# State-space heads of a two-block network: decay rows fetched from memory and differenced on GpSimd in place of a TensorE product and a ScalarE pass

## The reference

```python
a_cum = jnp.cumsum(a, axis=-1)                       # a = dt * A, per head, <= 0
seg = a_cum[..., :, None] - a_cum[..., None, :]
decay = jnp.exp(jnp.where(lower, seg, -jnp.inf))
y_diag = jnp.einsum('bcqgn,bcsgn,bgrcqs,bcsgrp->bcqgrp', cm, bm, decay, xs)
# + the part carried from the other chunk; then the same on the flipped sequence
y = y_fwd + y_bwd + d_skip[:, None] * xs
y = y * silu(z);  return rmsnorm(y, norm_w)
```

## Time and profile before

| what | value |
|---|---|
| median of 3 runs | 2441.19 us (2440.38 to 2445.71) |
| the profiled execution: its own time | 2443.01 us |
| its span | 2441.1 us |
| TensorE busy, mean granted clock | 2391.5 us (98%), 0.994 |
| VectorE, ScalarE, GpSimd busy | 1713.4, 1339.5, 90.2 us |

### The profile page before, as it was taken

One profiled execution on the slowest core, in us unless ns is written; L12 is line 12 of the kernel. 1 busy time (PEld: TensorE's weight loads), 2 busy tenths in 40 slices (PEclk: granted clock), 3 DMA queues, 4 the chain that ended last, 5 costly groups with the idle time before them and its releaser, 6 DMA issues.

```text
span 2441.1 us, 48177 instructions
## 1 busy us (share of the span) xinstructions
PE 2391.5 (98%) x18842; PEld 2289.4 (94%) x18842; DVE 1713.4 (70%) x2517; ACT 1339.5 (55%) x2355; POOL 90.2 (4%) x101
## 2 busy tenths in 40 slices
PE   9999999999999999999999999999999999999998
PEld 8898999999899999999999997899999999789998
DVE  7788777777888867786766575676566657667665
ACT  6788655644678855563444445554444444555443
POOL 0000000000100000000100010010001001001000
PEclk9999999999999999999999999999999999999999
DMA  7454555455354455545455553345545544434553
GB/s 216 131 159 126 165 164 161 154 170 189 108 153 139 137 156 160 169 155 181 145 181 174 169 160 106 121 144 178 170 147 179 178 163 152 123 124 142 189 181 113
DMA packets 401046, 380.19 MB, mean 156 GB/s; under 512 B 28223, under 2 KB 397037, under 8 KB 400765
## 3 DMA queue, kind: packets, MB, share of 16 engines
q1 hardware_dynamic: 397821, 373.87, 48.0%
q10 hardware_dynamic: 3072, 4.20, 0.7%
HBM read 372.77 MB, written 1.05 MB: 153 GB/s over the span
## 4 chain that ended last, share of the span: by engine, by line
PE 79%; DVE 12%; ACT 3%; DVEq 3%; issue 1%; SPq 1%; DMA 1%; ACTq 0%
PE ps L583 22%; PE ps L585 21%; PE ps L584 21%; DVE scratch L1806 3%; DVE w_lo L1583 3%; DVEq L1805 2%; PE ps L805 2%; PE ps L836 1%; PE ps L837 1%; PE ps L838 1%; ACT scratch L1082 1%; ACT w_hi L1082 1%; PE ps L854 1%; PE ps L612 1%; PE ps L614 1%
## 5 line engine op out<-in xcount | busy, mean ns | idle before, releaser
L1583 DVE TENSOR_TENSOR w_lo<-raw,w_hi 128x1024 fp32r<-128x1024 f32 x664 | 812.0, 1229 | 423.2 <-ACT w_hi L1082 421.8
L583 PE MATMUL ps<-x_hi,w_hi 128*128 128x256 f32 (+1 forms) x3664 | 1056.4, 288 | 4.3 <-DVE w_lo L1583 1.6
L584 PE MATMUL ps<-x_lo,w_hi 128*128 128x256 f32 (+1 forms) x3664 | 1042.6, 285 | 0.0
L585 PE MATMUL ps<-x_hi,w_lo 128*128 128x256 f32 (+1 forms) x3664 | 1039.8, 284 | 0.0
L1082 ACT ACTIVATE w_hi<-raw 128x1024 fp32r<-128x1024 f32 x664 | 697.7, 1056 | 447.5 <-PE ps L585 370.6
L583 PEld LDWEIGHTS ps<-x_hi,w_hi 128*128 128x128 f32 x3664 | 690.8, 189 | 30.8 <-issue 25.3
L584 PEld LDWEIGHTS ps<-x_lo,w_hi 128*128 128x128 f32 x3664 | 692.2, 189 | 2.0
L585 PEld LDWEIGHTS ps<-x_hi,w_lo 128*128 128x128 f32 x3664 | 693.6, 189 | 0.0
L583 PE MATMUL ps<-big_r,w_hi 128*128 128x272 f32 (+1 forms) x832 | 238.9, 287 | 0.0
L585 PE MATMUL ps<-big_r,w_lo 128*128 128x272 f32 (+1 forms) x832 | 238.2, 286 | 0.0
L1082 ACT ACTIVATE scratch<-ps 128x256 f32<-128x256 f32 (+9 forms) x328 | 122.3, 384 | 154.9 <-PE ps L838 63.8
(11 more groups left out here) (302 smaller groups left out, 3063.1 us busy)
## 6 DMA issues: line engine op xcount, KB each, us to landing
raw<-in_w_in SPq DMA_DIRECT2D x184, 512.0 KB, 4.7
raw<-in_ffn_w_up SPq DMA_DIRECT2D x176, 512.0 KB, 4.3
raw<-in_ffn_w_down SPq DMA_DIRECT2D x64, 512.0 KB, 4.2
raw<-in_mix_w_in SPq DMA_DIRECT2D x64, 512.0 KB, 4.6
scratch<-in_w_in SPq DMA_DIRECT2D x40, 512.0 KB, 4.8
raw<-in_w_mem_kv SPq DMA_DIRECT2D x32, 512.0 KB, 4.8
raw<-in_w_br_ssd SPq DMA_DIRECT2D x32, 512.0 KB, 3.8
raw<-in_ffn_w_down SPq DMA_DIRECT2D x32, 384.0 KB, 3.3
```

The lines of the kernel that those rows point to most:

```text
L583: mm(out, wh, xh, start=first, stop=False)
L584: mm(out, wh, xl, start=False, stop=False)
L585: return mm(out, wl, xh, start=False, stop=last)
L1583: tt(w_lo[:, p % PARTS, :, :], raw_at(slot_of(Q, p))[:, :, (p % 2) * P:(p % 2 + 1) * P], wh_f[:, p % PARTS, :, :], ALU.subtract).then_inc( ...
```

## The change

The row of a head no longer goes through TensorE, except for heads 0 and 1 of each layer. ScalarE copies the cumulated rows to SBUF in plain fp32, issues one transfer of them to a DRAM tensor `rows_dram`, and after each head's `decays` issues a transfer that reads the row of the head two later back into all 128 partitions (`even_row` or `odd_row`, 256 KB written). GpSimd forms the clamped differences of heads 2 to 31 with four `tensor_scalar` instructions per head (subtract a per-partition value, then min with 0), and ScalarE keeps only the Exp. The heads 0 and 1 of each later group are formed ahead, in a buffer of their own (`first_expo`), as soon as `decay` of the head two before is made. Heads 0 and 1 of a layer are spread in plain fp32 (two matmuls of 512 columns from 32 partitions). The remainders of the rows, the selector and GpSimd's clearing go. On VectorE the splits 11 and 12 move from before `x_dt` to after `weigh(0)` and `weigh(1)`, each later split moves by one step, and split 19 stands after `gate_y(3)`. GpSimd's sums of squares now stand between the heads: the first pair's after head 6 of its group, the other three's after head 1 of the next.

```diff
             for l in range(DEPTH):
                 pool.drain()
                 pool.memset(y_sum[:, :], 0.0)
+                pool.wait_ge(S["expo_ready"], l * SSD_HEADS + 2)
+                for h in range(2, SSD_HEADS):
+                    g, j = h // HEADS_PER_GROUP, h % HEADS_PER_GROUP
+                    pool.wait_ge(head_row_in[h % 2], 16 * (l * 15 + h // 2))
+                    pool.wait_ge(S["decay_ready"], l * SSD_HEADS + h - 1)
+                    for d, t, to, of in cuts:
+                        at = d * SSD_HEADS + h
+                        m = pool.tensor_scalar((first_expo if j < 2 else expo)[:, h % 2, to], (even_row, odd_row)[h % 2][:, of],
+                                               cum_tok[:, t, at:at + 1], 0.0, ALU.subtract, ALU.min)
+                    m.then_inc(S["expo_ready"], 1)
+                    if j == 6:
+                        add_square(l, 4 * g)
+                    if j == 1:
+                        for n in range(1, 4):
+                            add_square(l, 4 * (g - 1) + n)
...
                         cumulate()
+                        pe.wait_ge(S["row_ready"], l + 1)
                         pe.wait_ge(S["cum_ready"], l + 1)
-                        pe.wait_ge(S["row_ready"], l + 1)
-                        pe.wait_ge(S["rows_cleared"], l + 1)
-
-                    def spread_rows(j):
-                        if j >= 2:
-                            pe.wait_ge(S["expo_ready"], G * 8 + j - 1)
-                        h = g * HEADS_PER_GROUP + j
-                        sel = head_sel[:, h:h + 1].to_broadcast([P, P])
-                        mm(ps[2 + j % 2][:, :], sel, cum_rows[:, :], start=True, stop=True).then_inc(S["bc_done"], 1)
+                        for h in range(2):
+                            mm(ps[2 + h][:, :], const[0:SSD_HEADS, K_ID + h:K_ID + h + 1].to_broadcast([SSD_HEADS, P]), cum_rows[0:SSD_HEADS, :],
+                               start=True, stop=True).then_inc(S["first_rows"], 1)
...
-                    spread_rows(0)
-                    spread_rows(1)
                     for j in range(HEADS_PER_GROUP):
                         if j < 7 and (g or j >= 1):
                             proj(Q, T, 9 + j, 9 + j, x1)
-                        if j + 2 < HEADS_PER_GROUP:
-                            spread_rows(j + 2)
...
+                    def fetch_row(h):
+
+                        act.wait_ge(rows_out_done, 16 * (l + 1))
+                        act.wait_ge(S["expo_ready"], l * SSD_HEADS + h - 1)
+                        act.dma_start((even_row, odd_row)[h % 2][:, :], rows_dram[l, h].unsqueeze(0).to_broadcast([P, 2 * SEQ])).then_inc(head_row_in[h % 2], 16)
...
-                        copy(cum_rows[0:SSD_HEADS, :], ps[3][0:SSD_HEADS, :]).then_inc(S["row_hi"], 1)
+                        copy(cum_rows[0:SSD_HEADS, :], ps[3][0:SSD_HEADS, :]).then_inc(S["row_ready"], 1)
+                        act.wait_ge(S["row_ready"], l + 1)
+                        act.dma_start(rows_dram[l], cum_rows[0:SSD_HEADS, :]).then_inc(rows_out_done, 16)
                         copy(cum_tok[:, :, :].rearrange("p t h -> p (t h)"), ps[2][:, 0:2 * 64]).then_inc(S["cum_ready"], 1)
...
                     def decays(j):
 
-                        act.wait_ge(S["bc_done"], G * 8 + j + 1)
-                        for d, t, to, of in cuts:
-                            at = d * SSD_HEADS + g * HEADS_PER_GROUP + j
-                            m = fn(expo[:, j % 2, to], ps[2 + j % 2][:, of], ACT.Relu, scale=-1.0, bias=cum_tok[:, t, at:at + 1])
-                        m.then_inc(S["expo_ready"], 1)
-                        act.drain()
                         if j >= 4:
                             act.wait_ge(S["y_done"], G * 8 + j - 3)
-                        fn(decay[:, j % 4, :], expo[:, j % 2, :], ACT.Exp, scale=-1.0).then_inc(S["decay_ready"], 1)
+                        if g == 0 and j < 2:
+                            act.wait_ge(S["first_rows"], 2 * l + j + 1)
+                            for d, t, to, of in cuts:
+                                at = d * SSD_HEADS + j
+                                m = fn(expo[:, j % 2, to], ps[2 + j][:, of], ACT.Relu, scale=-1.0, bias=cum_tok[:, t, at:at + 1])
+                            m.then_inc(S["expo_ready"], 1)
+                            act.drain()
+                            fn(decay[:, j % 4, :], expo[:, j % 2, :], ACT.Exp, scale=-1.0).then_inc(S["decay_ready"], 1)
+                        else:
+                            act.wait_ge(S["expo_ready"], G * 8 + j + 1)
+                            fn(decay[:, j % 4, :], (first_expo if j < 2 else expo)[:, j % 2, :], ACT.Exp).then_inc(S["decay_ready"], 1)
+                        if g * HEADS_PER_GROUP + j + 2 < SSD_HEADS:
+                            fetch_row(g * HEADS_PER_GROUP + j + 2)
...
                     split(Q, 10)
-                    split(Q, 11)
-                    split(Q, 12)
-                    if g == 0:
-                        v.wait_ge(S["row_hi"], l + 1)
-                        tt(cum_rows[SSD_HEADS:2 * SSD_HEADS, :], ps[3][0:SSD_HEADS, :], cum_rows[0:SSD_HEADS, :].bitcast(F32),
-                           ALU.subtract).then_inc(S["row_ready"], 1)
...
                     for j in range(HEADS_PER_GROUP):
-                        if j < 7:
-                            weigh(j)
-                        if j == 6:
-                            weigh(7)
+                        for h in ((0, 1), (), (2,), (3,), (4,), (5,), (6, 7), ())[j]:
+                            weigh(h)
                         for t in ((), (0, 1), (2,), (3,), (), (), (), ())[j]:
                             z_silu_tile(t)
-                        if j:
-                            split(Q, 12 + j)
+                        split(Q, 11 + j)
                         if j in (3, 5, 7):
                             gate_y((j - 3) // 2)
                     gate_y(3)
+                    split(Q, 19)
```

More of the change, by code:

```diff
@@ L205, in build @@
         cum_tok = sb("cum_tok", [P, 2, 64])
-        head_sel = sb("head_sel", [P, SSD_HEADS], F32R)
+        odd_row = sb("odd_row", [P, 2 * SEQ])
+        rows_dram = nc.dram_tensor("cum_rows_dram", (DEPTH, SSD_HEADS, 2 * SEQ), F32, kind="Internal").ap()
         norm_bias = sb("norm_bias", [P, KT])
@@ L285, in build @@
         expo = view(scratch, 0, 2, 768)
+        first_expo = view(gates, 4608, 2, 768)
+        cuts = ((0, 0, slice(0, 256), slice(0, 256)), (0, 1, slice(256, 384), slice(128, 256)),
+                (1, 0, slice(384, 512), slice(256, 384)), (1, 1, slice(512, 768), slice(256, 512)))
         xbc = cut(6, SEQ)
@@ L338, in build @@
         rot_in = [sem("q_rotated_in"), sem("k_rotated_in")]
+        head_row_in = [sem("even_head_row_in"), sem("odd_head_row_in")]
+        rows_out_done = sem("cum_rows_written")
         wr = [sem(f"weights_in{i}") for i in range(RAW + 1)]
@@ L538, in _, with add_square @@
             pool.sem_inc(S["skip_ready"], 1)
-            with pool.Fori(0, DEPTH) as l:
+            def add_square(l, n):
                 pool.drain()
-                pool.memset(cum_rows[2 * SSD_HEADS:P, :].bitcast(F32), 0.0).then_inc(S["rows_cleared"], 1)
+                pool.wait_ge(S["y_squared"], l * 16 + n + 1)
+                pool.tensor_tensor(y_sum[:, :], y_sum[:, :], y_sq[:, n % 2, :], ALU.add).then_inc(S["sq_added"], 1)
+            for l in range(DEPTH):
                 pool.drain()
                 pool.memset(y_sum[:, :], 0.0)
-                with pool.Fori(0, 4 * GROUPS // 2) as p:
-                    for t in range(2):
-                        pool.drain()
-                        pool.wait_ge(S["y_squared"], l * 16 + p * 2 + t + 1)
-                        pool.tensor_tensor(y_sum[:, :], y_sum[:, :], y_sq[:, t, :], ALU.add).then_inc(S["sq_added"], 1)
+                pool.wait_ge(S["expo_ready"], l * SSD_HEADS + 2)
[13 more added lines that the diff above has]
+                            add_square(l, 4 * (g - 1) + n)
+                for n in range(1, 4):
+                    add_square(l, 4 * (GROUPS - 1) + n)
                 add_bias(l, SEQ)
@@ L1170, in small_params @@
                 fn(neg_a[:, :, :], neg_a[:, :, :], ACT.Exp).then_inc(S["nega_exp"], 1)
-                copy(head_sel[2 * SSD_HEADS:P, :], const[2 * SSD_HEADS:P, K_ID:K_ID + SSD_HEADS])
-                for r in (0, SSD_HEADS):
-                    m = copy(head_sel[r:r + SSD_HEADS, :], const[r:r + SSD_HEADS, K_ID + r:K_ID + r + SSD_HEADS])
-                m.then_inc(S["sel_ready"], 1)
                 act.wait_ge(S["lam_dot"], 1)
```

9 lines of the change are left out of this document (4 added, 5 removed).

## The result

The changed kernel takes 2553.8 us (median of 4, 2550.9 to 2556.7) against 2441.6 us for the kernel before on the same chip: ratio 1.0455, 95% interval 1.0443 to 1.0467. It is 4.5% slower. I had forecast 2433, with 2421 to 2467 as the range: both the number and the range were wrong, and so was the side that I leaned to.

What follows compares the result with a forecast made beforehand. TensorE, busy 98%, was taken as the bound with VectorE close behind. Six steady groups gave -12.0 us, two first groups +4.0, sum -8.0: 2443.0 - 8.0 - 1.8 = 2433.2 us, range 2421 to 2467.

Steps and rivals of the forecast that it cites:

- What the heads now cost: GpSimd's differences: 0.38 and 0.25 us an instruction, 1.26 us a head, 3.4 us with blocking by VectorE.
- GpSimd and VectorE become the bound, slower: Rival, heads 3 to 7 of every tail: at 4.1 us a head +25.6 us, 2467; upper price 2486; chance 0.28.
- The lower price of the prediction's estimate: GpSimd's `tensor_scalar` priced from below like a memset: 1.04 us a head, 3.2 us with blocking.
- two signs of being wrong: Prediction wrong if a head takes GpSimd over 3.7 us, or if the fetch, not GpSimd, ends ScalarE's wait.
- The blocking: GpSimd's four instructions per head must let one VectorE `weigh` (0.91 us) and one split (1.22 us) pass.
- The formula: Pair 3 starts 5.75 + 6P after a steady tail's start, summed over six steady and two first groups.
- P: GpSimd's time for one head's differences including blocking by VectorE: taken as 3.4 us, 3.2 to 4.5 with other prices.
- The fetch: Row transfer for head j+2 lands in 2.5 us; hidden behind GpSimd if it lands within about 3.3 us.
- the late case: Rival, the fetch is late: rows land at 4.3 us, +16.5 us, 2458; chance 0.10.
- What TensorE loses: Steady groups: 2.0 us of spread rows and pair 0's stall go; best tail to pair 3 24.9 us, 3.2 gained.
- A layer's first group: Heads 0 and 1 still through PSUM, nothing worked ahead: pair 3 2.0 us later, +4.0 us over two layers.
- The chain of who waits: L805's wait for `weigh` moves from pair 0 to pairs 1 and 3; ScalarE waits for GpSimd at its Exp.

Runs made afterwards that it cites:

- experiments 5 to 7: Changed kernel with other GpSimd forms for the differences: constant operand 2520.9 us, one operation 2528.1 us, sum of two tensors 2479.6 us.
- experiment 11: Changed kernel with the weighing's mask (`cb`) held in two PSUM banks, leaving the weighing one SBUF operand: 2524.6 us, ratio 1.0339.
- experiment 1: Changed kernel with GpSimd's four `tensor_scalar` per head replaced by memsets of zero of the same size: 2422.0 us, ratio 0.9904.
- three-fold zeros: Changed kernel with memsets of zero for GpSimd's differences, each head's zeros written three times, row transfers kept: 2457.2 us, ratio 1.0045.
- constant operand: Changed kernel with GpSimd's subtrahend a constant 0.0 in place of the per-partition value, both operations kept: 2520.9 us, ratio 1.0311.
- one operation: Changed kernel with GpSimd's instruction reduced to the smaller of row and per-partition value, without the subtraction: 2528.1 us, ratio 1.0348.
- five-fold zeros: Changed kernel with memsets of zero for GpSimd's differences, each head's zeros written five times: 2531.5 us, ratio 1.0363.
- experiment 7: Changed kernel with one sum of two tensors (row plus spread token value) in place of GpSimd's subtraction and clamp: 2479.6 us, ratio 1.0141.
- experiment 3: Kernel before with only the changed kernel's order of VectorE's work (later splits), complete computation: 2429.8 us, ratio 0.9943.

## Why the prediction was wrong

**The step that failed is the price of GpSimd's instruction.** In "What the heads now cost" I took 0.38 and 0.25 us, "nearer the memset", because it reads one tensor, and put the upper bound at the sum of two tensors, 2.3 us a head. Measured: 1.13 and 0.71 us, 3.67 us a head. The own price was 2.9 times what I took and 1.4 us above the bound, so the range could not hold the result. The bound rested on a thought about inputs, not on a row: no row showed this form, and the number of inputs turned out not to order the prices (experiments 5 to 7). I had named the mechanism, "GpSimd and VectorE become the bound, slower", and gave it 0.28; with a bound that allows a dearer form it would have been the forecast. The lower price of the prediction's estimate (one input near line rate, 768 columns in 1.04 us) isn't borne out either: that is 0.8 ns a column, and the form takes 3.4. Of the prediction's two signs of being wrong, a head over 3.7 us and a fetch that ends ScalarE's wait, the first came.

**The blocking was roughly right, one way.** I took 0.91 + 1.22 = 2.13 us a head; it is 5.21 - 3.67 = 1.5, of which the weighing's part is 0.7 (experiment 11). The other way round it is small beside this form. From `gate_y` at L1860's 0.89 us I concluded that VectorE waits for GpSimd too. That row was read rightly: all eight gates of the kernel before that begin 0.13 us after a sum of squares take 0.89 us. But beside a `tensor_scalar` that began 0.10 us earlier and runs for another 1.04 the same gate takes 0.65. In the tails of the changed kernel the splits' mean is 1254 ns (1219 in experiment 1), the longest 1.42 us, and the weighing's 1003 (955). The means over the whole run hide this, since few splits stand in the tails:

```profile
L1603 DVE TENSOR_TENSOR w_lo<-raw,w_hi 128x1024 fp32r<-128x1024 f32 x664 | 815.0, 1233 | 399.6 <-ACT w_hi L1095 398.1
...
L1866 DVE TENSOR_TENSOR big<-big,scratch 128x768 f32<-128x768 f32 x64 | 63.7, 1003 | 130.9 <-ACT big L1092 130.4
```

The exclusion that I quoted from the Trainium skill ("SBUF — State Buffer", "Who interferes with whom") is borne out for GpSimd's side. For VectorE's side the runs show it in full only beside GpSimd's sums of two tensors (0.43 to 0.89 us here, splits of 1.53 us in the kernel with the sum of two tensors); beside `tensor_scalar` VectorE is held for a part of the instruction. Why the two forms differ was not tested.

**The formula had the right slope and no term for the clock.** It says 2441.2 + 48P - 171 (P over 3.2). Against the measured times, with P from the traces:

- three-fold zeros, 3.9 by the loop: 2457 by the formula, 2457.2 measured; TensorE busy 9 us more than in experiment 1
- sum of two tensors, 4.2 by the loop, (3.51 + 0.33 + 4.55) / 2: 2472, 2479.6; 11 us more
- mask in PSUM, 4.50: 2486, 2524.6; 27 us more
- constant operand, 4.62: 2492, 2520.9; 29 us more
- one operation, 4.64: 2493, 2528.1; 27 us more
- five-fold zeros, 4.7: 2496, 2531.5; 31 us more
- the changed kernel, 5.21: 2520, 2553.8; 33 us more

It is right within 8 us for the first two, and 29 to 39 us short for the others. All run the same TensorE instructions as experiment 1, so the extra busy time is slower matmuls. For the changed kernel the formula's tail is right: 5.75 + 6 x 5.21 = 37.0 us, and its six steady tails are 37.6 to 38.1. What it lacks stands mostly behind pair 3. From pair 3 to the start of the next tail, here for groups 1 and 2, first in the changed kernel and then before:

```profile
102.32:135.33 33.01, 31.57 (x245) 29.68 (x245) 26.28 (x44) 19.83 (x41) 10.36 (x10) 0.94 0.43 133
172.96:206.29 33.33, 32.08 (x245) 30.14 (x245) 26.28 (x44) 19.85 (x41) 10.35 (x10) 0.92 0.43 131
```

```profile
90.63:120.25 29.62, 29.27 (x246) 28.25 (x245) 25.00 (x43) 19.61 (x39) 2.71 (x3) 1.00 0.36 109
148.40:177.69 29.29, 29.12 (x246) 28.24 (x245) 25.01 (x43) 19.71 (x39) 2.70 (x3) 1.00 0.36 111
```

Six such stretches are 22 us longer, of the 34 that the formula is short. In these two TensorE is busy 2.3 and 3.0 us longer and stands 1.1 us longer each. So a stall is paid as idle time and once more as slow matmuls. What makes TensorE stand there, and the 12 us that lie elsewhere, were not isolated.

**The fetch** was taken too short, and its issue too long (0.33 us, not 0.6):

```profile
L1244 ACTq DMA_DIRECT2D odd_row<-cum_rows_dram x30: 326/326/367, 67.4 to 948.3; - x30
...
DMA to landing us min/median/max: 3.0/4.0/7.9
```

I took 2.5 and called 4.3 the late case. In the changed kernel it costs nothing within the tails, since P is longer still. But it bars the forecast even at my P: the kernel with the sum of two tensors has a P of 3.5, close to my 3.4, and takes 2479.6, because its rows land in 4.5 us and the loop makes 4.2 us a head; VectorE's own longer splits and weighings (experiment 7) may have a part in it, which was not separated. My test "as long as it lands within about 3.3 us" was the right one; the rows behind it were 64 KB on that queue and 256 KB on another.

**What TensorE loses was right.** 2.0 us of spread rows and the stall of 1.1 us at pair 0, for each steady group, make a tail of 24.9 us; experiment 1 has 25.1. Split up, the reordering gives the tail the 1.2 us that I had put on it and the spread rows 1.8 where I had 2.0 (experiment 3). That the reordering is still 14 of the 22 us comes from outside the steady tails, which I had not counted: 0.5 us before each next tail, and the first groups.

**A layer's first group** came out about as its sum says, with the wrong P: with 5.21 the sum puts pair 3 12.9 us later. First rows to pair 0 kept their pace (69.32 for pair 0 in layer 1, 70.56 before), and pair 3 starts at 102.32 where it started at 90.63, 11.7 us later; layer 2's first tail is 13.8 us longer.

**The chain of who waits** was right: pair 0's wait gone, pairs 1 to 3 wait for the weighing, ScalarE waits for GpSimd at its Exp.

## What to carry to other kernels

Price an instruction of an engine by a row of the same form on the same engine; where there is none, don't bound it by another form with more inputs, and let the forecast's range say so. Before moving work to an idle engine, write its rate for a unit beside the rate at which the bound needs units, with the price free: here the room was 3.7 us a head for everything, 1.5 of it went to blocking, and the instructions cost 3.67 alone. Look at both engines when you choose a form: the sum of two tensors is, of the forms that ran, the cheapest for GpSimd and the dearest for VectorE beside it. For a transfer into one of n buffers the test is (user's time + issue + landing) / n against the round, and removing the engine's own cost doesn't remove it. Undo a change in parts: its reordering alone was worth more than half of all that it could gain, and it needed neither the transfers nor the other engine.

## What the runs showed of the hardware that I had not expected

- GpSimd, float32, 128 partitions, 256 and 128 columns, uncontended: memset 0.31 and 0.21 us; sum of two tensors with one spread operand 0.61 and 0.40; one operation with a per-partition operand 0.92 and 0.60; two operations 1.14 and 0.71. The sum of two full tensors is 0.74 for 256. The form with a scalar operand is the dearest.
- When VectorE's instructions with two SBUF inputs meet GpSimd's `tensor_scalar`, GpSimd pays nearly all: 3.67 us became 5.2, while VectorE's splits in the tails grew by 3% and its weighings by 5%. Beside GpSimd's sums of two tensors VectorE pays too: 25% on the splits, 16% on the weighings. Beside memsets neither pays.
- An operand of VectorE's weighing moved from SBUF to PSUM saves 29 us of the whole, because it frees GpSimd, though the weighing gets longer (1.10 us in two parts, not 1.00). The second part, and not PSUM, seems to be what it costs: 512 columns take 687 ns with one operand in PSUM, and another product of 512 columns with both in SBUF takes 692 in the same kernel.
- A row spread by a transfer to all partitions, 256 KB from 2 KB of DRAM, lands in 3.0 to 7.9 us, median 3.1 to 5.2 by kernel and buffer, beside weight streams at a DMA share of about 0.5.
